# Gated delta rule in a one-core decoder step: norms taken into the decays as logarithms, the state read before the inverse, blocks turned on VectorE, the next chunk's keys multiplied first

## The reference

```python
q = l2norm(q) * GDN_DK ** -0.5        # l2norm(x) = x * rsqrt(sum(x * x) + EPS)
k = l2norm(k)
gc = cumsum(g)                        # g: log decay of each token and head
decay = exp(where(tri_incl, gc[i] - gc[j], -inf))
kb = k * beta
L = where(tri_strict, (kb @ k.T) * decay, 0)
Tm = inverse(eye + L)                 # unit lower triangular, by chunk
u_val = Tm @ (v * beta)
w_k = Tm @ (kb * exp(gc))
attn = where(tri_incl, (q @ k.T) * decay, 0)
# scan over the chunks, S is the 128x128 state of a head
v_new = u_val - w_k @ S
o = (q * exp(gc)) @ S + attn @ v_new
S = S * exp(gc[-1]) + (k * exp(gc[-1] - gc)).T @ v_new
# afterwards: yb = rmsnorm(o) * gain * silu(z)
```

## Time and profile before

| | us |
|---|---|
| median of 3 launches | 4740.4 (4732.26 to 4743.85) |
| profiled execution, its own time | 4705.97 |
| its span, first to last instruction | 4704.3 |
| `delta_prompt` in it, first to last instruction of all engines | about 1366.3 to 1855.3 |

### The profile page before, as it was taken

The page is one execution under the profiler, slowest core; times in us unless marked ns, Lnnn a source line. Parts: engine busy times, 40 slices in busy tenths (PEclk is TensorE's granted clock), DMA queues, the critical chain, the costliest instruction groups (busy, mean ns, idle before and its releaser), DMA issues. The chain is left out here.

```text
span 4704.3 us, 76013 instructions
## 1 busy us (share of the span) xinstructions
PE 4470.3 (95%) x29021; PEld 4334.1 (92%) x29021; DVE 3082.0 (66%) x5449; ACT 1162.5 (25%) x2078; POOL 2138.6 (45%) x1485
## 2 busy tenths in 40 slices
PE   8999999999979998999899979997999999999998
PEld 6999999899858888999899979997999999999998
DVE  4124550111237675344588889997999999999997
ACT  3101320111214332003222234332222212222222
POOL 0233232233122221334155558875666666666664
PEclk9999999999989998999999999998999999999999
DMA  6122222433541112444222239999999999999996
GB/s 192 48 63 77 91 98 95 111 110 96 166 137 37 46 51 68 137 138 134 96 86 78 69 130 361 360 348 321 339 349 354 341 339 351 335 344 344 354 319 241
DMA packets 578567, 911.76 MB, mean 194 GB/s; under 512 B 150536, under 2 KB 398344, under 8 KB 578245
## 3 DMA queue, kind: packets, MB, share of 16 engines
q1 hardware_dynamic: 430016, 422.36, 28.0%
q0 software_dynamic: 111744, 406.90, 24.1%
q10 hardware_dynamic: 36640, 80.36, 4.7%
HBM read 775.67 MB, written 133.84 MB: 193 GB/s over the span
## 5 line engine op out<-in xcount | busy, mean ns | idle before, releaser
L2601 PE MATMUL ea_banks<-h_high,ea_uT_high 128*128 128x336 f32 x2048 | 655.8, 320 | 23.2 <-ACT ea_coef L3523 13.5
L2601 PE MATMUL ea_banks<-h_high,ea_uT_low 128*128 128x336 f32 x2048 | 651.8, 318 | 0.0
L2601 PE MATMUL ea_banks<-h_low,ea_uT_high 128*128 128x336 f32 x2048 | 648.0, 316 | 0.0
L121 PE MATMUL p_in<-h_high,w_in_high 128*128 128x352 f32 x1536 | 495.5, 323 | 0.0
L121 PE MATMUL p_in<-h_low,w_in_high 128*128 128x352 f32 x1536 | 492.3, 321 | 0.0
L121 PE MATMUL p_in<-h_high,w_in_low 128*128 128x352 f32 x1536 | 491.9, 320 | 0.0
L2576 POOL DMA_INDIRECT ea_u_raw<-in_peer_v,gt_index x192 | 300.6, 1565 | 272.2 <-DVE h_low_plain L3638 210.4
L2601 PEld LDWEIGHTS ea_banks<-h_high,ea_uT_high 128*128 128x128 f32 x2048 | 387.8, 189 | 24.6 <-ACT ea_coef L3523 13.7
L2576 POOL DMA_INDIRECT yT<-in_peer_u,gt_index x256 | 329.3, 1286 | 141.2 <-DVE ex_dots L3632 41.4
L2601 PEld LDWEIGHTS ea_banks<-h_low,ea_uT_high 128*128 128x128 f32 x2048 | 387.6, 189 | 0.0
L2601 PEld LDWEIGHTS ea_banks<-h_high,ea_uT_low 128*128 128x128 f32 x2048 | 386.4, 189 | 0.0
(11 more groups left out here) (531 smaller groups left out, 11632.0 us busy)
## 6 DMA issues: line engine op xcount, KB each, us to landing
w_in_raw<-in_w_in SPq DMA_DIRECT2D x88, 512.0 KB, 3.8
ex_gate<-tmp_gates SPq DMA_DIRECT2D x64, 672.0 KB, 8.4
ea_u_raw<-in_peer_uT SPq DMA_DIRECT2D x66, 512.0 KB, 3.8
w_mb_raw<-in_peer_v SPq DMA_DIRECT2D x64, 512.0 KB, 8.4
ea_uT_low_plain<-in_peer_uT SPq DMA_DIRECT2D x62, 512.0 KB, 8.3
ex_lv_low_plain<-in_peer_v SPq DMA_DIRECT2D x62, 512.0 KB, 8.7
tmp_acts<-ea_coef ACTq DMA_DIRECT2D x64, 336.0 KB, 2.8
tmp_gates<-yT SPq DMA_DIRECT2D x28, 768.0 KB, 6.3
```

The source lines that it names most:

```text
L121: last = pe.matmul(banks[0:rows, n, 0:CH], a[:, kk, 0:rows], b[:, kk, chunk(n)], start=(kk == 0 and a is wt.high[s] and b is high), stop=( ...
L2601: last = pe.matmul(acts.banks[:, n, 0:CD], a[:, c, :], b[:, c, dense(n)], start=(c == 0 and a is acts.uT_high[s] and b is high), stop=(c = ...
```

## The change

All edits are in `delta_prompt`.

- The sums of squares are one column for each head (4 heads times q and k, `ones[:, 0:1]` as the moving side) in one small corner of a PSUM bank. ACT takes Ln of all 16 columns at once, and Exp of -0.5, 0.5 and -1 times it. A small matmul with `steps` (half the difference of neighbouring tokens) turns the logs of the key norms into steps that DVE adds to the log decays (`step_gates`), so that the decays hold the key norms. POOL makes four 128x8 products (`scale_tokens`), which take the place of the old scales. q and k themselves stay unscaled; the 128x512 roots, the 16 reciprocals and the 4 products of POOL are gone. The query norm enters in the output's norm.
- w is gone. PE multiplies keys and state in level 3 (`read_done`), ACT scales it (`keep_read`, 4 instructions for each group), POOL subtracts it from `v_in` (`take_read`), and v_new is one product with the inverse.
- DVE turns `inv` and `invT` in 32x32 blocks: after `invert_pairs` and after levels 1 to 4. PE's transposes of it remain only before level 6 (one for each group).
- The keys of chunk t+1 are multiplied before chunk t's growth, and its q-k product behind chunk t's inner part; DVE makes L, the pairs and their inverse of chunk t+1 between `add_state` and `add_output` of chunk t. `make_gates`, `weigh_beta` and `weigh_decay` of POOL come in another order, and POOL gets `chunk_turn(7)` and `scale_output(7)` ahead of the two `cut_weights`.

The diff, cut to its core:

```diff
@@ tensor
-                pe.matmul(B(g, 1), k["ones"][:, :], sq_q[g][:, :, :], start=True, stop=True).then_inc(m["q_summed"], 1)
+                for a, sq in enumerate((sq_q, sq_k)):
+                    for h in range(HG):
+                        at = g * HG + h
+                        last = pe.matmul(sums[:, a, at:at + 1], sq[g][:, h, :], k["ones"][:, 0:1], start=True, stop=True)
+                last.then_inc(m["summed"], 1)
+            def shift_logs(t):
+                pe.wait_ge(m["logged"], t + 1)
+                pe.matmul(shifts, steps[:, :], logs[:, 1, :], start=True, stop=True).then_inc(m["shifted"], 1)
...
+                if 1 < lv <= BLOCKS + 1:
+                    pe.wait_ge(m["inv_kept"], level_at(t, lv - 2, g, BLOCKS))
+                if lv == TOP:
+                    pe.wait_ge(m["back_kept"], 2 * t + g + 1)
...
                         if lv == 3:
+                            pe.wait_ge(m["L_ready"], n + 1)
+                            heads(B(g, 0), k_of(g, s), S_of(g)).then_inc(m["read_done"], 1)
+                        if lv == 4 and not last:
+                            differences(t + 1, g)
+                        if lv == TOP and not first:
...
+                            turn_output(n - 2, g)
+                    if lv < 3 and not last:
+                        sum_squares(t + 1, lv - 1)
+                    if lv == 3 and not last:
+                        shift_logs(t + 1)
...
                 for g in range(2):
                     pe.wait_ge(m["v_kept"], n + 1)
+                    if not last:
+                        multiply_keys(t + 1, g, 1 - s)
                     heads(B(g, 3), k_out[g], v_new[g]).then_inc(m["grow_done"], 1)
...
                     heads(B(g, 2), attnT[g], v_new[g]).then_inc(m["intra_done"], 1)
+                if not last:
+                    for g in range(2):
+                        pe.wait_ge(m["o_part"], 2 * t + g + 1)
+                        multiply_queries(t + 1, g, 1 - s)
@@ scalar
+                act.activation(logs[:, :, :], sums, ACT.Ln, bias=k["eps"][:, 0:1]).then_inc(m["logged"], 1)
...
+                act.activation(norms[:, :, :], logs[:, :, :], ACT.Exp, scale=-0.5)
+                act.activation(k_length[:, :], logs[:, 1, :], ACT.Exp, scale=0.5)
+                act.activation(k_power[:, :], logs[:, 1, :], ACT.Exp, scale=-1.0).then_inc(m["norms_made"], 1)
@@ gpsimd
+                pool.tensor_tensor(v_in[g][:, :, :], v_in[g][:, :, :], read[g][:, :, :], ALU.subtract).then_inc(m["v_ready"], 1)
...
             chunk_turn(chunks - 2, 0)
+            chunk_turn(chunks - 1, 1, last=True)
+            scale_output(chunks - 1, 1)
             for u in range(2):
                 cut_weights(pool, wt, u, 0, u, first=True)
@@ vector
+                dve.transpose(inv[g][:, :, :].rearrange("p h n -> p (h n)"),
+                              invT[g][:, :, :].rearrange("p h n -> p (h n)")).then_inc(m["inv_kept"], 1)
...
+                for lv in range(1, BLOCKS + 1):
+                    extend(t, lv, 0)
+                    turn_blocks(t, lv, 0)
+                    extend(t, lv, 1)
+                    turn_blocks(t, lv, 1)
+                    if lv == 1:
+                        keep_k_out(t, 0, s)
...
+                    keep_couple(t, lv + 1, 0)
+                    keep_couple(t, lv + 1, 1)
...
+                    for g in range(2):
+                        weigh_keys(t + 1, g)
+                    for g in range(2):
+                        pick_pairs(t + 1, g)
+                        add_state(t, g)
+                    for g in range(2):
+                        invert_pairs(t + 1, g)
+                    for g in range(2):
+                        turn_pairs(t + 1, g)
+                        add_output(t, g)
+                    for g in range(2):
+                        weigh_queries(t + 1, g)
```

More of the change, by code:

```diff
@@ L1715, in chunk_turn @@
                     n = 2 * t + g
[L1716 to L1733, removed]
+                    pe.wait_ge(m["invT_made"], n + 1)
                     if not first:
@@ L1766, in chunk_turn @@
[L1766 to L1767 removed]
                     n = 2 * t + g
[L1769 to L1772, removed]
[L1773 to L1778 removed]
+                    pe.wait_ge(m["invT_ready"], level_at(t, TOP - 1, g, NL - 1))
@@ new lines, in invert_output, with keep_read @@
+            def invert_output(t, first=False):
+                act.wait_ge(m["o_logged"], t + 1)
+                if not first:
+                    act.wait_ge(m["o_scaled"], t)
+                act.activation(o_inv[:, :], o_log[:, :], ACT.Exp, scale=-0.5).then_inc(m["o_inverted"], 1)
+            def keep_read(t, g, s, first=False):
+                n = 2 * t + g
+                act.wait_ge(m["read_done"], n + 1)
+                act.wait_ge(m["scaled"], t + 1)
+                if not first:
+                    act.wait_ge(m["v_ready"], n - 1)
+                for h in range(HG):
+                    at = g * HG + h
+                    done = act.mul(read[g][:, h, :], B(g, 0)[:, h, :], read_by[:, s, at:at + 1])
+                done.then_inc(m["read_kept"], 1)
@@ new lines, in chunk_turn @@
+            def chunk_turn(t, s, next_landed, first=False, last=False, second=False):
+                if not last:
+                    act.wait_ge(landed[1 - s], next_landed)
+                    for g in range(2):
+                        square(t + 1, g, 1 - s)
+                if not first:
+                    for g in range(2):
+                        square_output(t - 1, g, 1 - s)
+                if not last:
+                    take_logs(t + 1)
+                if not first:
+                    take_output_logs(t - 1)
+                if not last:
+                    make_norms(t + 1)
+                if not first:
+                    invert_output(t - 1, first=second)
+                for g in range(2):
+                    keep_read(t, g, s, first)
+                if not last:
+                    for g in range(2):
+                        raise_decays(t + 1, g)
@@ L1872, in chunk_turn @@
                     act.copy(v_new[g][:, :, :], B(g, 0)).then_inc(m["v_kept"], 1)
+            act.wait_ge(landed[0], 16)
+            for g in range(2):
+                square(0, g, 0)
+            take_logs(0)
+            make_norms(0, first=True)
             act.wait_ge(m["totalled"], 1)
@@ L1939, in _, with take_read, chunk_turn @@
-            gates(0, first=True)
+            def take_read(t, g):
+                n = 2 * t + g
+                pool.wait_ge(m["vrow_kept"], n + 1)
+                pool.wait_ge(m["read_kept"], n + 1)
+                pool.tensor_tensor(v_in[g][:, :, :], v_in[g][:, :, :], read[g][:, :, :], ALU.subtract).then_inc(m["v_ready"], 1)
+            def chunk_turn(t, s, first=False, last=False):
+                if not last:
+                    make_gates(t + 1)
+                if not first:
+                    scale_output(t - 1, 1 - s)
+                if not last:
+                    if not first:
+                        pool.wait_ge(m["o_scaled"], t)
+                    scale_tokens(t + 1, 1 - s)
+                    for g in range(2):
+                        weigh_beta(t + 1, g)
+                for g in range(2):
+                    take_read(t, g)
+                if not last:
+                    for g in range(2):
+                        weigh_decay(t + 1, g)
@@ new lines, in chunk_turn @@
+                extend(t, TOP - 1, 0)
+                extend(t, TOP - 1, 1)
+                if not first:
+                    norm_output(t - 1, 1)
+                keep_couple(t, TOP, 0)
+                keep_couple(t, TOP, 1)
+                extend(t, TOP, 0)
+                extend(t, TOP, 1)
+                if not first:
+                    for g in range(2):
+                        finish_output(t - 1, g, 1 - s, z_in, first=(kind == "second"))
+                for g in range(2):
+                    keep_state(t, g, s)
```

454 lines of the change are left out of this document (202 added, 252 removed).

## The result

The change made the kernel slower: 4772.7 us (median of 10, 4751.5 to 4795.0) against 4714.6 us for the kernel before on the same chip (median of 10, 4702.1 to 4744.2). The ratio is 1.0115, with a 95% interval of 1.0084 to 1.0146. Forecast was 4690 us, a gain of 50, with a range from 4665 to 4724; what came is a loss of 58.

A forecast was written before the change was run, and what follows sets the result against it. PE's instruction rate was taken to bound a chunk's inside; first grow to last product -49.8 us, start -4, end +3.8, total -50.0, so 4740.4 - 50 = 4690 us, with a range from 4665 to 4724.

The forecast's parts named there:

- Clock: Behind chunk borders: low-clock stretches follow PE waits, 4.5 us lost each; 20 us taken, bounds 0 and 36.
- rival 2: At every chunk border the clock falls: 36 us in place of 20, time 4706; chance 0.13.
- I take 0: One-column sums of squares on PE: no extra cost for failing to overlap, against 2.9 us more a chunk otherwise.
- rival 3: One-column products on PE don't overlap: 2.9 us for each of 7 chunks, 4710, chance 0.12; twice that, 4731, chance 0.05.
- if the granted clock stays low beyond the first levels: A sign that would show the prediction wrong: TensorE's low clock lasting past a chunk's first levels; no size given.
- The PE account and the period: PE's work per chunk falls from 50.1 to 44.0 us; with waits, the full-clock period from 54.0 to 47.5.
- The block turn: DVE's 32x32 turn of 512 columns priced like an elementwise instruction: 0.60 us apart, 0.68 long, hidden in levels 1 to 3.
- rival 1: VectorE becomes the bound through dear block turns; at the reciprocal's 3.76 us each, about 4870 us; chance 0.05.
- The border: Between chunks PE waits 1.5, 0.35 and 1.3 us for DVE's queue: 3.2 replacing most of the 3.9 before.
- the loop's return: DVE returns behind its last `weigh_queries`, costing 4 us, bounds 0 and 5.
- Start and end: Block start: first grow 4 us earlier, bounds -8 and +1. Block end: 3.8 us longer, from DVE held up, table loads, POOL's product.
- The tables: ACT loads two tables a chunk, for Ln and Exp; hidden inside the block, +2.6 us at its end.

The follow-up runs named there:

- The version with 128 columns: Changed kernel with its sum-of-squares products 128 columns wide instead of one: 4670.4 us, ratio 0.991 to the kernel before.
- the run above: Changed kernel with its one-column sums kept, plus three unread 512-column products a chunk in PE's border waits: 4722.2 us, ratio 1.0016 to the kernel before.
- the version with three products: Changed kernel with sums 128 columns wide, plus three unread 512-column products a chunk in PE's border waits: 4653.4 us, ratio 0.9889 to the kernel before.
- with the cuts early: Kernel with 128-column sums and three unread wide products a chunk, POOL's two `cut_weights` moved ahead of `scale_output(7)`: 4661.4 us, ratio 0.9893 to the kernel before.
- its twin: Kernel before with 32 unread product instructions more a chunk, behind the fillers of levels 1 and 2, 64 columns wide: 4751.9 us, ratio 1.009.

## Why the prediction was wrong

**The step that failed is "Clock".** It had the clock fall only behind a wait of PE, gave each low stretch 4.5 us from one row, and took 20 us with an upper bound of 8 x 4.5 = 36. The loss was 147 us in the block (34 before), so 113 more, where the sum had 4 more. That difference, 109, is as large as the whole miss between 50 faster and 58 slower. The version with 128 columns splits it: it loses 50 us to the clock, 16 more than before (give or take 5), and that goes with the new border's waits, near rival 2 (36 us in place of 16, so 20 more). The other 97, from 50 to 147, are the one-column products': a low stretch behind the border lasts 7 to 10 us with 128 columns and 30 to 45 with one.

**"I take 0" for the one-column products** was right as a distance and wrong as a cost. The prediction asked only whether they overlap. They do: at full clock eight instructions of one column take 0.82 us in the run above (1576.58 to 1577.40), against 0.85 for eight of `couple`; rival 3 (they don't overlap) is refuted. What was not asked is what 32 such instructions in each chunk do to TensorE's clock. No row of before held one, the nearest had 32 columns, and its clock was not looked at. Of the prediction's own signs of failure, "if the granted clock stays low beyond the first levels" is the one that came.

**The PE account and the period held.** Full-clock work fell by 58 us (455 to 397); the sum without its clock term was -54. In the version with three products the couples of chunks 2 and 3 start 48.4 us apart at a clock of 1.00, against 47.5 forecast. (It has wide products where the forecast has waits; the 128-column version's 51.6 us between chunks 2 and 3, less 3.4 for its low stretch, gives 48.2.)
```profile
1496.25 2.17 PE L1682 MATMUL dp_ps<-dp_invT,dp_L 128*128 128x64 f32 x16
...
1544.65 2.17 PE L1682 MATMUL dp_ps<-dp_invT,dp_L 128*128 128x64 f32 x16
```

**The block turn** was priced 0.60 apart and 0.68 long. Groups of the kernel after, by form:
```profile
L2090 DVE STREAM_TRANSPOSE dp_inv<-dp_invT 128x512 f32<-128x512 f32 x64 | 45.5, 711 | 2.2
L2067 DVE TENSOR_TENSOR dp_o<-dp_o,dp_o_r 128x512 f32<-128x512 f32 x16 | 19.7, 1238 | 5.1 <-POOL dp_o_r L1961 5.1
L1854 ACT ACT_TABLE_LOAD x8 | 10.3, 1283 | 0.1
L1864 ACT ACT_TABLE_LOAD x8 | 10.3, 1283 | 0.1
```
It is 711 ns long, and rival 1 (VectorE becomes the bound) has no support: DVE is busy 264 of 543 us.
The Trainium skill ("VectorE: DVE Perf Modes", The three transpose paths) had led to an estimate of 1.24 us; the trace has 0.71.

**The border** has its waits where they were forecast: 1.43 us for the first turned pair (forecast 1.5) and up to 1.00 for R (forecast 1.3). Inside the levels no wait exceeds 0.24 us. At the loop's return PE stands for 3.76 us in all, where the forecast had 4 on top of the border's waits.

**Start and end.** Both terms came out worse than forecast, 7 us together. The first grow starts 38.7 us behind the block's first product (before 37.6), where -4 was forecast. The start runs at the lower level, but that is not all of it: with 128 columns it takes 36.8. From the last product to the cast that opens the next stage pass 19.0 us against 13.0 before: +6.0, with +3.8 forecast. Norm and cut met (4.25 us for the pair); with the cuts early the same stretch takes 16.4.

**The tables.** One load of 1283 ns stands before each Ln (L1854) and each Exp (L1864), 8 of each, and 2 and 2 for the output norm. The prediction counted so. The Trainium skill ("ScalarE: Activation LUTs", Table sets: the hidden batching unit) would have had none between Exp and Ln; the trace disagrees, 20 loads of 1283 ns in the block.

What stays open: why a product of one column does not always hold TensorE's clock, when its weights of 128x128 are loaded just as for 128 columns. No run separated the columns streamed from what else such a product lacks (results written, say). And it is not settled which waits start a low stretch: 1.69 us was followed by one in the kernel with one-column products added and not in its twin, and the same kernel's chunks 4 to 6 had none.

## What to carry to other kernels

Count what a small product does to the clock, not only what it takes. Here eight instructions of one column took 0.82 us and eight of 128 columns 0.89, so narrowness bought next to nothing; try such a product with its full 128 columns first. A short wait of PE inside a dense stretch is worth filling with a wide product that nobody reads; here three such products a chunk, 24 in all, made the block 23 us shorter. When PE's busy share rises while its instructions fall, read the granted clock of that stretch before anything else.

## What the runs showed of the hardware

- At one and the same busy share (20.00 of 20.00 us) TensorE ran at 0.51, and in another kernel 43.75 of 43.8 at 1.00: the level does not follow the busy time of the records.
- 16 instructions of one column were followed by the lower level (1.2 GHz) without a wait before them; 16 of 128 columns in the same place were not. Added to the kernel before, the same instructions left the level at 2.4 GHz in chunks 4, 5 and 6.
- A standstill of 2.87 us at the loop's return left the level at 2.4 GHz in the version with three wide products, while waits of 1.43 and 1.00 us were followed by 7 us at the lower level in the one without.
- A 32x32 block turn of 128x512 f32 on VectorE takes 711 ns; while POOL ran its 2.67 us subtraction, two DVE instructions that otherwise take 1.29 took 4.25.
